# Three plain norms: the first chunk behind each multiplies unnormalised halves, and the roots go on in the banks

## The chip, the cores and the metric

The kernel runs on one core of one Trainium2 chip. The metric is the device time of one execution in microseconds; lower is better.

## The reference

Two blocks of two layers each work on x (512 tokens, width 1024, float32). The first has a latent-attention and RWKV mixer, then a Mamba-2 mixer, each followed by a cross attention to a memory and a gated feed-forward; the second has two layers of a gated attention mixer and a convolved feed-forward. What matters here is the norm ahead of a projection:

```python
def rms_norm(x, g, eps=NORM_EPS):
    xf = x.astype(jnp.float32)
    y = xf * lax.rsqrt(jnp.mean(xf * xf, axis=-1, keepdims=True) + eps)
    return (y * g.astype(jnp.float32)).astype(x.dtype)

def swiglu_ffn(h, norm, w13, w2):
    u = rms_norm(h, norm) @ w13
    return (jax.nn.silu(u[..., :FFN_HIDDEN]) * u[..., FFN_HIDDEN:]) @ w2
```

The root belongs to a token, so it can be multiplied in before or behind the product with W. Three norms are touched: ffn_norm of layer 0 (site 1), od_norm ahead of the Mamba projection (site 2) and ffn_norm of layer 1 (site 3). They have a gain and no shift.

## The kernel before

x is kept transposed: eight tiles of 128 features by 512 tokens. Each projection is a Job, cut into chunks of up to 512 output columns (four tiles, four PSUM banks) and each chunk into slices of 128 input features. For every slice, weights and activations are split into a rounded high half and a low half, and TensorE (L417) runs three terms: high x high, low x high, high x low; with four tiles that is 12 matmuls. ScalarE rounds the weights (L436) four slices ahead of TensorE, once slice s-4 is done, and GpSimd makes their low halves (L440). Chunks take the two groups of four banks in turn; a chunk may start when the one before it in its group has given its banks back (`await_free`). A guest job (od_dt, 32 columns) is run in the middle of od_x, after slice 3 of its second chunk, in the bank group of the first.

What else belongs to a job is its Finish: generators for ScalarE and VectorE. `Stream.walk` writes the order of each queue: at every slice it first rounds weights (ScalarE only), then takes two steps of the pending Finish generators, then one step of a `beside` generator. At the first slice of a job with flush=0 all that is pending is written out first. The queues are in order, so a wait holds up all behind it.

A plain norm (class Rms) follows a job that adds into x (AddToX, chunks of 512, 256 and 256 columns). VectorE adds each tile to x (L987), ScalarE squares it (L703), VectorE folds the squares of tiles 0 to 5 into one (L724). The last chunk is "rushed": tiles 6 and 7 are added and squared by halves (L708). When the job ends, TensorE sums the folded squares (L738) and the halves (L715) with a matrix of ones, runs filler matmuls (`keep_busy`, L239), and transposes the roots so that they stand in a bank as a row for every partition (L746), with more filler behind. Between them VectorE averages (L798), ScalarE takes the root (L753) and VectorE inverts it (L2283 to L2291). VectorE then scales tile after tile by gain and row (L821, L825), ScalarE rounds (L760, L772), VectorE takes the low half (L781); the next job's first chunk follows tile by tile.

The job behind sites 1 and 3 is ffn_up0 (class Gated, eight slices a chunk): ScalarE's sigmoids (L1974), VectorE's products with the banks (L1986, L1991), the rounding (L1979) and the low half (L1995) of the result. After that VectorE has a "rider" with each chunk, a product of mod_w with a vector (L1039 and seven L1044), which TensorE turns by four transposes (L1064) after slice 5 of the next chunk. Behind site 2 come od_x (class Mixed: ScalarE L2104, then twelve taps of a convolution on VectorE, L2123, which read the banks) and its guest od_dt. The xo job ahead of sites 1 and 3 has four slices a chunk, the down job ahead of site 2 has ten.

RowsLater is an older relative: the norm of the cross attention multiplies raw halves, rounded at L848 and with the low half at L852.

## Time and profile before

| | us |
|---|---|
| median of 3 runs | 3366.26 (3365.47 to 3368.86) |
| profiled execution | 3368.29 |
| its span | 3366.4 |
| TensorE busy | 3304.4 (98%) |
| VectorE busy | 1763.8 (52%) |
| ScalarE busy | 1435.9 (43%) |
| GpSimd busy | 1492.0 (44%) |
| mean granted TensorE clock | 0.997 of full speed |

The busy times come from the page of the profile. TensorE's holds its filler and its sums too. The timeline lists the instructions of all engines in order of time, equal neighbours merged, with the idle time ahead of them in brackets.

### The profile page before, as it was taken

How to read it: one execution, taken by the hardware profiler on the slowest of the kernel's cores; microseconds unless marked ns; L12 is line 12 of the kernel's file. 1: busy time of each engine (PE TensorE's matmuls, PEld its weight loads, DVE VectorE, ACT ScalarE, POOL GpSimd, SP SyncE). 2: the span in 40 equal slices, each digit the busy share in tenths (PEclk: the TensorE clock that was granted, in tenths of full speed). 3: DMA queues.
4: the chain of work that ended last, by engine and by line, in shares of the span. 5: the costliest groups of instructions: out<-in, count | busy, mean ns of one | idle time of the engine just before them, and what ended most of it. 6: DMA issues, size and time to landing. Idle time of an engine off the chain costs nothing. (4 is left out here: it accounts for less than half of the span.)

```text
span 3366.4 us, 48377 instructions
## 1 busy us (share of the span) xinstructions
PE 3304.4 (98%) x19096; PEld 2724.3 (81%) x19096; DVE 1763.8 (52%) x3073; ACT 1435.9 (43%) x2918; POOL 1492.0 (44%) x1353
## 2 busy tenths in 40 slices
PE   9999999999998999999999999999999999999999
PEld 7769788888886788888888877888888877888887
DVE  4765675636456664656353376445153186545143
ACT  4662354323355554532333337344343246444343
POOL 3330254454443545354544443445554443444543
PEclk9999999999999999999999999999999999999999
DMA  4210024545221123354533220232323220123331
GB/s 124 75 57 4 27 88 151 194 144 192 85 88 51 42 97 100 101 169 163 170 125 117 82 77 11 75 100 86 102 85 103 92 82 26 51 89 99 100 94 56
DMA packets 233851, 317.79 MB, mean 94 GB/s; under 512 B 8877, under 2 KB 151196, under 8 KB 233628
## 3 DMA queue, kind: packets, MB, share of 16 engines
q1 hardware_dynamic: 204982, 260.50, 24.1%
q10 hardware_dynamic: 28646, 54.22, 4.7%
q8 instruction: 152, 2.49, 0.3%
q14 instruction: 71, 0.58, 0.1%
HBM read 312.59 MB, written 2.10 MB: 93 GB/s over the span
## 5 line engine op out<-in xcount | busy, mean ns | idle before, releaser
L417 PE MATMUL banks<-split,split 128*128 128x512 f32 (+2 forms) x11760 | 2675.2, 388 | 8.1 <-ACT split L436 3.7
L417 PEld LDWEIGHTS banks<-split,split 128*128 128x128 f32 x11760 | 2183.7, 188 | 476.5 <-issue 15.7
L440 POOL TENSOR_TENSOR split<-kept,split 128x512 fp32r<-128x512 f32 (+3 forms) x1174 | 1363.8, 1166 | 1581.1 <-ACT split L436 1578.6
L436 ACT ACTIVATE split<-kept 128x512 fp32r<-128x512 f32 (+3 forms) x1174 | 648.9, 559 | 1436.4 <-PE banks L417 1389.3
L2047 DVE SCALAR_TENSOR_TENSOR work<-banks,kept,work 128x511 f32<-128x511 f32 (+1 forms) x176 | 120.4, 745 | 257.1 <-ACT work L2029 256.3
L1044 DVE SCALAR_TENSOR_TENSOR work<-work,kept 128x512 f32<-128x512 f32 x168 | 195.5, 1164 | 6.0
L989 DVE SCALAR_TENSOR_TENSOR kept<-banks,kept 128x512 f32<-128x512 f32 (+1 forms) x56 | 34.3, 669 | 207.8 <-PE banks L417 207.8
L987 DVE TENSOR_TENSOR kept<-banks,kept 128x512 f32<-128x512 f32 (+1 forms) x72 | 41.1, 625 | 193.2 <-PE banks L417 193.2
L613 DVE COPY work<-banks 128x512 f32<-128x512 f32 (+1 forms) x64 | 37.4, 643 | 187.9 <-PE banks L417 187.9
L1986 DVE TENSOR_TENSOR work<-work,banks 128x512 f32<-128x512 f32 x44 | 28.3, 684 | 165.5 <-ACT work L1974 165.5
L1673 ACT ACTIVATE work<-work 128x128 f32<-128x128 f32 (+3 forms) x160 | 89.5, 560 | 47.0 <-DVE work L1733 46.1
L2123 DVE SCALAR_TENSOR_TENSOR work<-banks,kept,work 128x511 f32<-128x511 f32 (+2 forms) x72 | 49.5, 742 | 58.9 <-ACT work L2104 58.4
L239 PE MATMUL banks<-kept 128*128 128x128 f32 x438 | 60.2, 290 | 12.4 <-PEq L266 10.2
L1600 PE MATMUL banks<-kept,work 128*128 128x128 f32 x400 | 71.0, 275 | 0.6 <-ACT work L1673 0.6
L1733 DVE CUSTOM_DVE_ANT_0 work<-banks,kept 128x128 f32<-128x128 f32 (+3 forms) x96 | 46.8, 487 | 41.6 <-PE banks L1888 21.1
L239 PEld LDWEIGHTS banks<-kept 128*128 128x128 f32 x438 | 55.9, 204 | 15.4 <-issue 13.0
L724 DVE TENSOR_TENSOR work<-work 128x512 f32<-128x512 f32 x66 | 64.0, 969 | 7.5 <-ACT work L703 2.1
L1616 PE MATMUL banks<-work 128*64 128x128 f32 x592 | 61.1, 283 | 0.8 <-DVE work L1744 0.5
L2029 ACT ACTIVATE work<-banks,kept 128x512 f32<-128x512 f32 x88 | 60.9, 771 | 0.0
L1600 PEld LDWEIGHTS banks<-kept,work 128*128 128x128 f32 x400 | 48.7, 140 | 14.9 <-issue 6.2
L3871 PE MATMUL banks<-kept 64*64 64x64 f32 (+1 forms) x1408 | 55.4, 233 | 1.9 <-DVE kept L4106 1.4
L3871 PEld LDWEIGHTS banks<-kept 64*64 64x64 f32 x1408 | 53.0, 134 | 3.5 <-DVE kept L4106 3.5
(460 smaller groups left out, 3106.7 us busy)
## 6 DMA issues: line engine op xcount, KB each, us to landing
work<-in_mod_w ACTq DMA_DIRECT2D x48, 1024.0 KB, 6.5
kept<-in_ffn_w SPq DMA_DIRECT2D x94, 512.0 KB, 4.9
kept<-in_w_up SPq DMA_DIRECT2D x88, 512.0 KB, 4.7
kept<-in_w_in SPq DMA_DIRECT2D x36, 1024.0 KB, 5.0
kept<-in_od_w_in SPq DMA_DIRECT2D x19, 1024.0 KB, 5.2
kept<-in_ffn_w SPq DMA_DIRECT2D x18, 1024.0 KB, 5.4
kept<-in_w_down SPq DMA_DIRECT2D x18, 1024.0 KB, 5.2
kept<-in_ev_w_in SPq DMA_DIRECT2D x8, 1024.0 KB, 5.2
```

The costliest lines, as they stand in the source:

```text
L239: pe.matmul(self.PS[:, bank, 0:P], self.ident, self.ones, start=True, stop=True)
L417: m = pe.matmul(self.bank(q, j), lhs, rhs, start=t == 0 and i == 0, stop=t == job.KT - 1 and i == 2)
L436: act.activation(self.weights(s, 0), self.source(s), ACT.Copy).then_inc(self.rounded, 1)
L440: pool.tensor_tensor(self.weights(s, 1), self.source(s), self.weights(s, 0), ALU.subtract).then_inc(self.k.slices_split, 1)
L724: dve.tensor_tensor(total, total, self.square_at(t), ALU.add).then_inc(self.folded, 1)
L1044: ins = dve.scalar_tensor_tensor(out=self.sum, in0=self.slot[:, t, :], scalar=self.x[:, t:t + 1], in1=self.sum, op0=ALU.mult, op1=ALU.add)
L1600: m = pe.transpose(self.bank(self.TB[u % 2])[:, c * P:(c + 1) * P], self.prob[u % 4][:, c * P:(c + 1) * P], self.k.ident)
L1616: ins = pe.matmul(self.o_bank(h // 2)[i * 64:i * 64 + 64, t * P:(t + 1) * P], self.heads[h + i].v(c), self.probT[(u + i) % 3][:, c * P:(c ...
L1673: act.activation(tile, tile, ACT.Exp, bias=self.top[:, u % 8:u % 8 + 1], scale=-1.0, accum_out=self.total[:, u % 16:u % 16 + 1]).then_inc( ...
L2029: act.activation(self.cv[:, j, :], self.stream.bank(q, j), ACT.Identity, bias=col(self.k, f"conv_b_2{self.l}", at), scale=col(self.k, f"co ...
L2047: return dve.scalar_tensor_tensor(out=v, in0=self.stream.bank(q, j)[:, 0:S - lag], scalar=col(self.k, f"conv_w_2{self.l}{2 - lag}", self.c ...
L3871: m = pe.matmul(PS[half, bank, q * P:q * P + n], lhs(q)[half], rhs(q)[half], start=start, stop=stop)
```

## The change

The three norms become RawFirst. In AddToX each tile of x is now also rounded with its gain and without the root, and VectorE takes its low half; all eight squares are folded, the last chunk is no longer rushed, and nothing of the norm stands between the jobs. The first chunk of the next job multiplies the raw halves. Behind its slice 1 TensorE sums the folded squares, behind slice 3 it transposes the roots, and ScalarE copies the row from its bank to SBUF. From slice 4 on VectorE scales x by gain and that row, ScalarE rounds and VectorE takes the low half, two tiles a slice, for the later chunks; scaling tile t waits until slice t has been multiplied. VectorE multiplies the four finished banks of the first chunk by the row, and the Finish reads them after that. At site 2 the raw halves have places of their own (the low ones where the scaled x goes), and the guest waits for the normed halves. At its core:

```diff
-            terms = (whi, hi(t)), (wlo, hi(t)), (whi, lo(t))
+            high, low = finish.operands(c, hi, lo)
+            terms = (whi, high(t)), (wlo, high(t)), (whi, low(t))
...
+        elif c == 1 and self.raw_first():
+            self.after.await_normed_high(pe, t)
     def ready_low(self, pe, c, t):
         if self.after and c == 0:
             self.after.await_half(pe, t)
+        elif c == 1 and self.raw_first():
+            self.after.await_normed_half(pe, t)
+    def raw_first(self):
+        return isinstance(self.after, RawFirst)
+    def operands(self, c, hi, lo):
+        return self.after.raw if c == 0 and self.raw_first() else (hi, lo)
+    def even_out(self, dve, q, j):
+        bank = self.stream.bank(q, j)
+        self.stream.await_tile(dve, q, j)
+        if j == 0:
+            dve.wait_ge(self.after.kept, 1)
+        dve.tensor_tensor(bank, bank, self.after.row, ALU.mult).then_inc(self.after.evened, 1)
+    def await_even(self, eng, q, c, j):
+        if c == 0 and self.raw_first():
+            eng.wait_ge(self.after.evened, j + 1)
+        else:
+            self.stream.await_tile(eng, q, j)
...
+class RawFirst(Rms):
+    SUM, ROOT, SPREAD, SCALE = 1, 1, 3, 4
+    def __init__(self, k, T, src, gain, halves, squares_at, n_squares, rows_at, tmp, n_tmp, dim, raw=None):
+        super().__init__(k, T, src, gain, halves, squares_at, n_squares, rows_at, tmp, n_tmp, dim)
+        self.raw = raw or halves
+        self.row = self.sq[:, n_squares - 1, :]
+    def signals(self, st):
+        super().signals(st)
+        self.kept, self.evened = st.signals(2)
+    def round(self, act, t):
+        act.activation(self.raw[0](t), self.src(t), ACT.Identity, scale=self.gain(t)).then_inc(self.rounded, 1)
+    def rest(self, dve, t):
+        dve.wait_ge(self.rounded, t + 1)
+        dve.scalar_tensor_tensor(out=self.raw[1](t), in0=self.src(t), scalar=self.gain(t), in1=self.raw[0](t), op0=ALU.mult,
+                                 op1=ALU.subtract).then_inc(self.halved, 1)
+    def used_by(self, stream, job, bank):
+        self.stream, self.bank_at = stream, bank
+        self.slice0 = next(s for s, one in enumerate(stream.slices) if one[1] is job)
+    def beside(self, pe, t):
+        if t == self.SUM:
+            self.sum_folded(pe, self.k.PS[:, self.bank_at, :])
+        if t == self.SPREAD:
+            self.spread_roots(pe, self.k.PS[:, self.bank_at + 1, :])
+    def normed_round(self, act, t):
+        act.wait_ge(self.scaled, t + 1)
+        act.activation(self.hi(t), self.tmp(t % self.n_tmp), ACT.Copy).then_inc(self.rounded, 1)
+    def normed_rest(self, dve, t):
+        dve.wait_ge(self.rounded, self.T + t + 1)
+        dve.tensor_tensor(self.lo(t), self.tmp(t % self.n_tmp), self.hi(t), ALU.subtract).then_inc(self.halved, 1)
+    def normed_scale(self, dve, t):
+        self.stream.await_slice(dve, self.slice0 + t)
+        if t >= self.n_tmp:
+            dve.wait_ge(self.halved, self.T + t - self.n_tmp + 1)
+        dve.scalar_tensor_tensor(out=self.tmp(t % self.n_tmp), in0=self.src(t), scalar=self.gain(t), in1=self.row,
+                                 op0=ALU.mult, op1=ALU.mult).then_inc(self.scaled, 1)
+    def scalar_beside(self, act):
+        for _ in range(self.slice0):
+            yield
+        for i in range(self.SCALE + self.T // 2 + 1):
+            if i == self.ROOT:
+                self.root_of(act)
+            if i == self.SPREAD:
+                act.wait_ge(self.spread, 1)
+                act.activation(self.row, self.rows, ACT.Copy).then_inc(self.kept, 1)
+            for t in range(2 * (i - self.SCALE), min(2 * (i - self.SCALE + 1), self.T)):
+                if t >= 0:
+                    self.normed_round(act, t)
+            yield
+    def vector_beside(self, dve, link):
+        for _ in range(self.slice0):
+            yield
+        for i in range(self.SCALE + self.T // 2 + 1):
+            if i == self.ROOT:
+                self.roots(dve, link)
+            if i == self.SCALE:
+                dve.wait_ge(self.kept, 1)
+            for t in range(2 * (i - self.SCALE), 2 * (i - self.SCALE + 1)):
+                if 0 <= t < self.T:
+                    self.normed_scale(dve, t)
+                if 1 <= t <= self.T:
+                    self.normed_rest(dve, t - 1)
+            yield
+    def await_normed_high(self, eng, t):
+        eng.wait_ge(self.rounded, self.T + t + 1)
+    def await_normed_half(self, eng, t):
+        eng.wait_ge(self.halved, self.T + t + 1)
...
+        self.raw = isinstance(rms, RawFirst)
+        self.folded = rms.T if rms_later or self.raw else self.FOLDED
         if rms:
             rms.fold_first(self.folded)
-            rms.by_halves = not rms_later
+            rms.by_halves = not rms_later and not self.raw
...
-        if self.rms and not self.rms_later and c == len(self.job.widths) - 1:
-            eng.wait_ge(self.rms.scaled, self.rms.T)
+        if self.rms and c == len(self.job.widths) - 1:
+            if self.raw:
+                eng.wait_ge(self.rms.kept, 1)
+            elif not self.rms_later:
+                eng.wait_ge(self.rms.scaled, self.rms.T)
...
+                self.rms.round(act, self.first(c) + j)
+                yield
...
+                self.rms.rest(dve, self.first(c) + j)
+                yield
...
+            self.after.beside(pe, t)
...
+                self.even_out(dve, q, j)
+            yield
...
+    stream = Stream(k, [(xo, AddToX(k, rms=rms), *o_halves), *ffn_jobs(k, plan, l, rms, rms_next), *tail],
+                    HALVES_AT, opened=Opened.N, beside=Besides([rms, *([rms_next] if l == 0 else [])]))
+    rms.used_by(stream, up, stream.free_banks(xo))
+    if l == 0:
+        rms_next.used_by(stream, plan["od_x"], stream.free_banks(down))
+    stream.run()
```

A new `Besides` steps the RawFirst generators (two in layer 0, one in layer 1) once a slice. In AddToX the new steps (round, rest) come behind the adds, squares and folds of each chunk.

## Rows read from the trace of the kernel before

**Rows 1.** The page: busy time (x instructions), and the costliest line with its idle.

```profile
PE 3304.4 (98%) x19096; PEld 2724.3 (81%) x19096; DVE 1763.8 (52%) x3073; ACT 1435.9 (43%) x2918; POOL 1492.0 (44%) x1353
...
L417 PE MATMUL banks<-split,split 128*128 128x512 f32 (+2 forms) x11760 | 2675.2, 388 | 8.1 <-ACT split L436 3.7
```

**Rows 2.** Timeline, site 1: start, us, engine line op out<-in xcount [idle <-releaser].

```profile
526.67 1.05 PE L738 MATMUL banks<-kept,work 128*128 128x128 f32 x8
...
527.56 1.95 PE L715 MATMUL banks<-kept,work 128*128 128x128 f32 x16
...
530.80 0.65 PE L746 MATMUL banks<-kept,work 128*128 128x128 f32 x4
...
531.29 1.28 PE L239 MATMUL banks<-kept 128*128 128x128 f32 x10
...
532.69 27.48 PE L417 MATMUL banks<-split,split 128*128 128x512 f32 x120
```

**Rows 3.** Timeline around site 2.

```profile
897.93 1.05 PE L738 MATMUL banks<-kept,work 128*128 128x128 f32 x8
...
903.95 46.42 PE L417 MATMUL banks<-split,split 128*128 128x512 f32 x203
```

**Rows 4.** Timeline: VectorE at an earlier raw norm (437), then ahead of site 1.

```profile
437.18 12.74 DVE L852 SCALAR_TENSOR_TENSOR split<-kept,split 128x512 fp32r<-128x512 f32 x8
...
515.31 2.48 DVE L987 TENSOR_TENSOR kept<-banks,kept 128x512 f32<-128x512 f32 x4 [11.48 <-PE banks L417]
...
518.84 1.84 DVE L724 TENSOR_TENSOR work<-work 128x512 f32<-128x512 f32 x2 [0.46 <-DVE work L724]
...
521.20 1.29 DVE L987 TENSOR_TENSOR kept<-banks,kept 128x512 f32<-128x512 f32 x2 [0.52 <-PE banks L417]
...
523.06 0.62 ACT L436 ACTIVATE split<-kept 128x512 fp32r<-128x512 f32 x1
...
528.67 1.27 POOL L440 TENSOR_TENSOR split<-kept,split 128x512 fp32r<-128x512 f32 x1 [0.35 <-ACT split L436]
```

**Rows 5.** Timeline: scalings of the first chunk at site 1.

```profile
533.32 0.74 DVE L825 SCALAR_TENSOR_TENSOR work<-kept,banks 128x512 f32<-128x512 f32 x1
...
534.58 0.74 DVE L825 SCALAR_TENSOR_TENSOR work<-kept,banks 128x512 f32<-128x512 f32 x1
```

**Rows 6.** Timeline behind the first chunk of site 1.

```profile
554.77 0.63 ACT L436 ACTIVATE split<-kept 128x512 fp32r<-128x512 f32 x1 [2.09 <-PE banks L417]
...
557.35 1.28 DVE L1986 TENSOR_TENSOR work<-work,banks 128x512 f32<-128x512 f32 x2 [15.59 <-ACT work L1974]
...
558.55 1.27 DVE L1991 TENSOR_TENSOR work<-work,banks 128x512 f32<-128x512 f32 x2
...
561.14 1.53 DVE L1039 TENSOR_SCALAR work<-work,kept 128x512 f32<-128x512 f32 x1
562.70 8.28 DVE L1044 SCALAR_TENSOR_TENSOR work<-work,kept 128x512 f32<-128x512 f32 x7
...
571.13 0.63 PE L1064 MATMUL banks<-kept,work 128*128 128x128 f32 x4
```

**Rows 7.** Timeline behind the first chunk of site 2.

```profile
926.54 2.77 ACT L2104 ACTIVATE work<-banks,kept 128x512 f32<-128x512 f32 x4
...
927.33 8.26 DVE L2123 SCALAR_TENSOR_TENSOR work<-banks,kept,work 128x511 f32<-128x511 f32 x12 [14.32 <-ACT work L2104]
```

**Rows 8.** PE's timeline; a stretch: us, busy by engine, PEclk, DMA share, GB/s.

```profile
40.41 5.47 PE L417 MATMUL banks<-split,split 128*128 128x512 f32 x12
...
1064.65 0.41 PE L4385 MATMUL banks<-split,split 128*128 128x384 f32 x1 [2.62 <-issue]
...
1067.00:1068.00 1.00, 1.00 (x12) 1.00 (x12) 1.00 (x3) 0.00 (x0) 0.00 (x0) 0.51 0.07 16
...
1139.32 1.58 PE L239 MATMUL banks<-kept 128*128 128x128 f32 x12 [2.45 <-PEq L266]
1140.65 5.71 PE L417 MATMUL banks<-split,split 128*128 128x512 f32 x24
```

More of the change, by code:

```diff
@@ L358, in __init__, with free_banks @@
             self.done_by.append(whole)
+    def free_banks(self, job):
+        last = self.first_chunk(job) + len(job.widths) - 1
+        assert job.tiles(len(job.widths) - 1) <= 2
+        return self.groups[last] * 4 + 2
     def first_chunk(self, job):
@@ new lines, with __init__, signals, scalar @@
+class Besides(Part):
+    def __init__(self, norms):
+        self.norms = norms
+    def signals(self, st):
+        pass
+    def scalar(self, act, q, c):
+        works = [norm.scalar_beside(act) for norm in self.norms]
+        while any([next(work, 0) is None for work in works]):
+            yield
+    def vector(self, dve, link, q, c):
+        works = [norm.vector_beside(dve, link) for norm in self.norms]
+        while any([next(work, 0) is None for work in works]):
+            yield
+    def more(self, block):
+        pass
@@ L923, in rushes @@
     def rushes(self, c):
-        return self.rms is not None and not self.rms_later and c == len(self.job.widths) - 1
+        return self.rms is not None and self.rms.by_halves and c == len(self.job.widths) - 1
     def await_free(self, eng, c):
         eng.wait_ge(self.added, self.first(c + 1) + (self.job.tiles(c) if self.rushes(c) else 0))
-        if self.rms and not self.rms_later and c == len(self.job.widths) - 1:
-            eng.wait_ge(self.rms.scaled, self.rms.T)
+        if self.rms and c == len(self.job.widths) - 1:
[3 more added lines that the diff above has]
+                eng.wait_ge(self.rms.scaled, self.rms.T)
         if self.rider and c == 0:
@@ L946, in tensor_end @@
             self.rms.sums_bank = self.sums_bank()
-        elif self.rms:
+        elif self.rms and not self.raw:
             q2 = self.stream.first_chunk(self.job) + 2
@@ L972, in scalar @@
             yield
+        if self.raw:
+            for j in range(self.job.tiles(c)):
+                self.rms.round(act, self.first(c) + j)
+                yield
         if self.rider and c == 0:
@@ L976, in scalar @@
             yield from self.rms.finish_scalar(act)
-        if self.rms and not self.rms_later and c == len(self.job.widths) - 2:
+        if self.rms and self.rms.by_halves and c == len(self.job.widths) - 2:
             act.activation(self.k.idle, self.k.ones[:, 0:1], ACT.Sqrt)
@@ L996, in vector @@
                 yield
+        if self.raw:
+            for j in range(self.job.tiles(c)):
+                self.rms.rest(dve, self.first(c) + j)
+                yield
         if self.rider and c == 0:
             yield from self.rider.vector(dve, link, self.RIDES, self.k.PS[:, q % 2 * 4, :])
-        if self.rms and c == len(self.job.widths) - 1:
+        if self.rms and not self.raw and c == len(self.job.widths) - 1:
             yield from self.rms.finish_vector(dve, link)
@@ L1960, in tensor @@
     def tensor(self, pe, c, t):
+        if c == 0 and self.raw_first():
+            self.after.beside(pe, t)
         if c >= 1 and t == self.job.KT - 3:
@@ L1983, in vector @@
     def vector(self, dve, link, q, c):
+        if c == 0 and self.raw_first():
+            for j in range(4):
+                self.even_out(dve, q, j)
+            yield
         for p in range(2):
@@ L2113, in scalar, with tensor @@
                 yield
+    def tensor(self, pe, c, t):
+        if c == 0 and self.raw_first():
+            self.after.beside(pe, t)
     def vector(self, dve, link, q, c):
+        if c == 0 and self.raw_first():
+            for j in range(4):
+                self.even_out(dve, q, j)
+            yield
         for lag in range(1, 4):
@@ L2940, in cross_attention @@
            opening=[opening], beside=mem, closing=[attend], idle_first=0 if l == 0 else 6, early=SLOTS if l == 0 else 1).run()
-    rms = x_norm(k, lambda t: col(k, f"ffn_norm{l}", t), split_tiles(k, A_WORK, A_H), at=HID_AT + 8 * S)
+    rms = x_norm(k, lambda t: col(k, f"ffn_norm{l}", t), split_tiles(k, A_WORK, A_H), at=HID_AT + 8 * S,
+                 raw=True)
     if l == 0:
-        rms_next = x_norm(k, lambda t: col(k, "od_norm", t), odd_halves(k), dst=k.H)
+        rms_next = x_norm(k, lambda t: col(k, "od_norm", t), odd_halves(k), dst=k.H, raw=split_tiles(k, A_WORK, A_H))
         xbc = k.view(A_WORK, XBC // P, S)
@@ L2948, in cross_attention @@
         mixed = Mixed(k, xbc, SCRATCH_AT + 7 * S, after=rms_next, flush=0)
-        tail = [(plan["od_x"], mixed, *h), (plan["od_dt"], Steps(k, dt, tmp, cum, odd_spread(k), at_tile(43), at_tile(59)), *h),
+        tail = [(plan["od_x"], mixed, *h), (plan["od_dt"], Steps(k, dt, tmp, cum, odd_spread(k), at_tile(43), at_tile(59), rms_next), *h),
                 (plan["od_xbc"], Mixed(k, xbc, SCRATCH_AT + 7 * S, tile0=8, before=mixed), *h)]
@@ L2974, in split_tiles, with x_norm @@
     return lambda t: hi[:, t, :], lambda t: lo[:, t, :]
-def x_norm(k, gain, halves, shift=None, at=SCRATCH_AT, dst=None, n_squares=4):
+def x_norm(k, gain, halves, shift=None, at=SCRATCH_AT, dst=None, n_squares=4, raw=None):
     if dst is None:
@@ L2983, in x_norm @@
         tmp, n_tmp = (lambda i: dst[:, i, :]), DT
+    if raw:
+        return RawFirst(k, DT, lambda t: k.X[:, t, :], gain, halves, at, n_squares, at + n_squares * S, tmp, n_tmp, D,
+                        raw=None if raw is True else raw)
     return Rms(k, DT, lambda t: k.X[:, t, :], gain, halves, at, n_squares, at + n_squares * S, tmp, n_tmp, D, shift=shift)
@@ L4189, with __init__ @@
 class Steps(Finish):
-    def __init__(self, k, dt, tmp, cum, spread, rest_at, rounded_at, after=None, flush=None):
-        self.k, self.after, self.flush, self.spread_with = k, after, flush, spread
+    def __init__(self, k, dt, tmp, cum, spread, rest_at, rounded_at, normed):
+        self.k, self.normed, self.spread_with = k, normed, spread
         self.dt, self.tmp, self.cum = (v[0:SSM_H, :] for v in (dt, tmp, cum))
@@ L4199, in signals, with ready, ready_low @@
         self.freed, self.begun, self.bent = st.signals(3)
+    def ready(self, pe, c, t):
+        self.normed.await_normed_high(pe, t)
+    def ready_low(self, pe, c, t):
+        self.normed.await_normed_half(pe, t)
     def scalar(self, act, q, c):
```

10 lines of the change are left out of this document (4 added, 6 removed).

## The prediction

> **What bounds the kernel now.** The page first: TensorE is busy 98% of the span, and its main line, L417, waits 8.1 us in 11760 matmuls [rows 1]. So time can only be won where TensorE does something that the reference doesn't need, and lost where it is made to wait. Then the timeline around the first norm that the change touches (site 1, ffn_norm0). The last matmul of the output projection gives way to the sum of the folded squares at 526.67, the half sums start at 527.56, the spreading transposes at 530.80, filler at 531.29, and the next chunk's first matmul comes at 532.69 [rows 2]. That is 6.02 us in which TensorE sums, spreads and runs filler. Site 2 (od_norm) has the same gap, 897.93 to 903.95 [rows 3], and site 3 (ffn_norm1) repeats it at 1414.64 to 1420.67. A slice of 12 matmuls costs 2.72 us (120 in 27.48, less the drain of the last [rows 2]). Last, the timeline of the first chunk behind each site, for what VectorE owes when that chunk ends; here lies the answer.
>
> **What goes.** At each site TensorE no longer stands between two jobs: 3 x 6.02 = 18.1 us. It keeps the folded sum, 527.56 - 526.67 = 0.89, now behind slice 1 of the chunk, and the four transposes, 531.29 - 530.80 = 0.49 [rows 2], now behind slice 3: 1.38 a site. **Gross gain 3 x 4.64 = 13.9 us.** The Sqrt behind the averages loses the early load of its table, but from the end of the sums to the transposes the whole root takes about 1.3 us now [rows 2], and two slices, 5.4 us, lie between them after the change: free, and it would cost something only if it grew fourfold. The raw halves of tiles 0 to 5 are made while the projection still runs, so slice 0 can start at once.
>
> **What comes in, before the boundary (sites 1 and 3).** VectorE gets a second subtraction per x tile (8 of the form of L852) and two more folds. The xo job has only four slices a chunk, so its last two chunks last 10.9 us. I lay VectorE's queue out for site 1: the four adds start at 515.31 and take 0.62 each, the folds 0.92 each beside GpSimd [rows 4], which ends them at 520.7 (as now). New: four raw rests. Alone such an operation takes 0.74 (L825's form [rows 5]); beside a GpSimd that never pauses L852 takes 12.74 / 8 = 1.59 [rows 4]. GpSimd works here on 256-wide slices with pauses, so I take 1.0, nearest to the folds of this place: 524.7. Only then the adds of tiles 4 and 5, to 526.0 (now they are done by 522.5). ScalarE squares tile 5 by 526.6, and only then rounds the chunk's first weights, which now happens at 523.06 [rows 4]. TensorE wants them at 526.67: about 1.0 us late, part of it for the low half, which GpSimd makes in 1.27 more [rows 4]. Behind that, two folds, two rests, two adds and the last two folds end near 533.2, against TensorE's arrival at the sum at 533.1. So 1.0 us a site. Bounds: 0.2 with every rest at 0.74; 4.9 with every rest and fold at 1.6. Site 2 has ten slices a chunk: the same work ends 7 us before the boundary, and tiles 6 and 7 are folded by +4 us (even at the 1.6 us price) against an arrival at +5.4: nothing.
>
> Operations of VectorE that read two tensors of SBUF stretch beside GpSimd (1.59 against 0.74 [rows 4, 5]), while those with a bank as source stay at 0.69 to 0.74 (L825 [rows 5], L2123 [rows 7]). The new scaling reads its row from SBUF, the old one read it from a bank. The Trainium skill's SBUF — State Buffer, "Who interferes with whom", speaks here against the change: a VectorE instruction with two SBUF inputs and a GpSimd one that reads SBUF exclude each other for a whole instruction. By that rule the scalings join the exposed kind; on the path are scale 6 and 7, 2 x 0.85 = 1.7 a site if GpSimd runs beside both, and nothing by the rows of the bank.
>
> **What comes in, behind the boundary (sites 1 and 3).** Eight scalings and eight low halves, now done while TensorE runs the chunk itself, move to slices 4 to 8. Two scalings and two roundings go with a slice, and ScalarE rounds only after it has seen slice t end, so tiles 0 to 5 are ready by the chunk's end, about 0.6 us ahead of it: free. Call that end E; at site 1 now E = 532.69 + 8 x 2.72 = 554.45. VectorE is idle from there to its first gating product at 557.35, E+2.9 [rows 6]; the four new products of a bank with the row of roots, 0.62 to 0.65 each by the adds' rows [rows 4], fit: free. They sit ahead of the sigmoids only by one tile each, and ScalarE's table load covers that.
> Not free is what the order puts next: scale 6, rest 5, scale 7, rest 6 between the gating products and the second products at 558.55, and rest 7 ahead of the mod_w work of the rider (L1039 at 561.14, L1044). A scaling with its rest takes 1.26 now (533.32 to 534.58 [rows 5]); GpSimd is mostly idle in that moment, since ScalarE, waiting for VectorE, hands it nothing. Two pairs are 2.5, with 0.3 for the exchange with ScalarE, rest 7 0.7 to 0.8: **3.6 us later**. The rider's eight products now run from 561.14 to 570.98, and TensorE's L1064, which needs their sum, starts at 571.13, when the chunk's sixth slice has ended at 554.45 + 6 x 2.72 = 570.77, plus a little: the two arrive within 0.3 us of each other [rows 6]. There is no slack. 3.6 us of VectorE turn into 3.6 us of TensorE at site 1 and again at site 3 (the same rows recur at 1459.09). Bounds: 0 if the rider should wait for something that is not late; 7.5 if all five, at 1.6 (+3.9), collide. The delay ends there: the rider would be through by about 575, and the next chunk, whose work VectorE waits for then, ends some 5 us later.
>
> **Site 2.** No rider, but the od_dt guest wants chunk 0's banks after three slices plus one of chunk 1, at E + 4 x 2.72 = E+10.9, and takes them when VectorE's twelve taps are through. E = 903.95 + 21.76 = 925.71. Now the taps start at E+1.6 and end at 935.59, E+9.9 [rows 7]: slack 1.0. After: the four bank products end at E+2.2, so the taps start 0.6 later, two pairs come in after the first two taps (2.9 with the exchange), rest 7 after six (0.7): +4.2, **3.2 us of waiting**. Bounds: 2.5 (pairs at 1.26 and no exchange) and 5.5 (four of five at 1.3 to 1.6).
>
> **The sum.** 13.9 - 2 x 1.0 - 2 x 3.6 - 3.2 = **1.5 us faster**; against the profiled execution, 3368.29 (span 3366.4 and 1.9 around it), that is 3366.8. The profiled execution lies 2.0 above the median of 3366.26, which becomes **3364.8**. A measurement of this kernel tells some 0.2%, 6.7 us, from no change.
>
> **Rivals.**
> A. The rider isn't late: the pairs hide in VectorE's waits for ScalarE, or TensorE's own 1 us of lateness covers them. For it: VectorE idles 2.9 us behind E. Against it: that idle time is spent before the pairs are reached, by the order of the queue. Gain 13.9 - 2.0 - 3.2 = 8.7, or 3357.6. If nothing is late anywhere, 13.9: 3352.4.
> B. The pre-boundary queue at GpSimd's full price: 4.9 in place of 1.0, twice: 1.5 - 7.8 = -6.3, or 3372.6. For it: L852's eight rows. Against it: GpSimd's pauses, and the folds' 0.92 in this very stretch.
> C. The clock falls in the new waits; this ends on the slower side. Now the boundary is filled with matmuls; the new waits of 3.2 to 3.6 us are bare. The bare wait of 2.45 is followed by full rate (24 matmuls in 5.71 [rows 8]); the one of 2.62, in sparse work, is followed by a granted clock of 0.51, that is 1.2 GHz in place of 2.4 [rows 8]. At that level 12 matmuls took 5.47 in place of 2.72: 2.75 lost [rows 8]. My waits lie just above the longest that is known to be harmless. Three falls cost 8.3: 1.5 - 8.3 = -6.8, or 3373.1. It turns the sign from one such fall on, and it passes 0.2% when three come or when two come with B. The page TensorE: Matmul & The Clock Gate of the Trainium skill ("What's actually happening") describes two levels granted by recent activity; rows 8 agree, and my price is theirs.
>
> **How the numbers follow.** Forecast 0.50 (own range 3361 to 3369: the two unknown rates of VectorE), A 0.15 and nothing late 0.05, B 0.12, C 0.18, of which two thirds pass 0.2%. Faster by over 0.2%: A, nothing late, and a little of the forecast's edge, 0.22. Slower: 0.12 of C and a little of B, 0.13. The same: 0.65. The range leaves out nothing late, half of C's far side and what lies past B: 3357 to 3373.5.
>
> **What would show it.** At each site L417 follows L417 without L715 or L239 between, and L738 comes after 24 more matmuls. Right: waits of L417 for L436 or L440 near 1 us at the first slice of the up0 job; the L1064 of the first rider 3 to 4 us late, released by L1044; the first guest matmul 3 us late, released by L2123. Wrong: L1064 on time (A), granted clock under 1.0 in the slices after a wait (C), the scalings at 0.74 beside GpSimd (the port does not matter), or a wait at the transposes (the root chain is not free).

## The result, and the profile after

| | before | after |
|---|---|---|
| median, same chip | 3366.65 us (5 runs) | 3380.93 us (5 runs, 3379.22 to 3384.7) |
| profiled execution | 3368.29 | 3379.22 |
| its span | 3366.4 | 3377.4 |
| mean granted TensorE clock | 0.997 | 0.995 |

The ratio is 1.0041 [1.0029, 1.0052]: 14.3 us slower, where 1.5 us faster was forecast, and outside the range. The direction was wrong too. The profiled executions differ by 11.0 us of span.

The page after, lines that answer to [rows 1]:

```profile
PE 3298.0 (98%) x18982; PEld 2712.5 (80%) x18982; DVE 1815.7 (54%) x3106; ACT 1448.7 (43%) x2933; POOL 1499.9 (44%) x1353
...
L424 PE MATMUL banks<-split,split 128*128 128x512 f32 (+2 forms) x11760 | 2683.5, 389 | 13.0 <-DVE work L2292 4.5
```

L424 is the old L417. The same 11760 matmuls are busy 8.3 us longer (2683.5 against 2675.2) and wait 4.9 us longer. The mean clock, 0.995 against 0.997, hardly moves, but the busy time of unchanged work hints at a lower clock, and the stretches below show it. The waits of TensorE, by line and releaser (sum, times, longest), hold three large entries that belong to the change:

```profile
PE banks L1219 <- DVE work L1199: 10.6, 2, 5.3
...
PE banks L424 <- DVE work L2292: 4.5, 1, 4.5
...
PE banks L771 <- DVE work L757: 2.3, 2, 1.2
```

L1219 is the rider (old L1064) at sites 1 and 3, L424 behind L2292 the guest at site 2, L771 (old L738) the sum of the folded squares. TensorE's timeline at site 1, to be held against [rows 2, 6]:

```profile
501.46 23.12 PE L424 MATMUL banks<-split,split 128*128 128x512 f32 x100
524.94 4.84 PE L424 MATMUL banks<-split,split 128*128 128x512 f32 x20 [0.36 <-POOL split L447]
530.95 1.16 PE L771 MATMUL banks<-kept,work 128*128 128x128 f32 x8 [1.17 <-DVE work L757]
531.86 5.72 PE L424 MATMUL banks<-split,split 128*128 128x512 f32 x24
537.42 0.60 PE L779 MATMUL banks<-kept,work 128*128 128x128 f32 x4
537.77 27.48 PE L424 MATMUL banks<-split,split 128*128 128x512 f32 x120
570.54 1.09 PE L1219 MATMUL banks<-kept,work 128*128 128x128 f32 x4 [5.29 <-DVE work L1199]
571.28 19.05 PE L424 MATMUL banks<-split,split 128*128 128x512 f32 x72
```

The gap of 6 us is gone: L424 follows L424 over the boundary (it lies in the row of 501.46), with the sum and the transposes between its slices. What came in stands in the brackets (0.36, 1.17, 5.29), and in the last row: 72 matmuls in 19.05, where six slices should take about 16.3. The stretches of one microsecond around the end of the rider's wait say why (busy share and count for PE, PEld, DVE, ACT and POOL, then PEclk, the granted clock; the last two numbers are the DMA's):

```profile
569.00:570.00 1.00, 0.00 (x0) 0.00 (x0) 1.00 (x1) 0.00 (x0) 0.85 (x1) 0.83 1.03 393
570.00:571.00 1.00, 0.46 (x3) 0.49 (x4) 0.40 (x1) 0.15 (x1) 0.00 (x0) 0.50 1.08 356
...
573.00:574.00 1.00, 1.00 (x4) 0.71 (x4) 0.00 (x0) 0.00 (x0) 0.00 (x0) 0.50 1.08 373
...
577.00:578.00 1.00, 1.00 (x6) 0.83 (x5) 0.00 (x0) 0.36 (x1) 0.57 (x1) 1.00 0.00 0
```

The clock falls in the last microsecond of the wait (0.83 is the mean of a stretch in which it fell), stays at 0.50 (1.2 GHz), with four matmuls a microsecond, and is back at 1.00. It is rival C: the wait, and then the clock. The Trainium skill's page TensorE: Matmul & The Clock Gate ("What's actually happening") describes just these two levels, with the lower one granted after TensorE was idle; the trace agrees, 0.50 behind the wait of 5.29 and 1.00 before and after.

VectorE at site 1, around the end of the first chunk, shows why the rider waits. E, counted as in the prediction, is 537.77 + 4 x 2.72 = 548.65. L956 is the scaling (here of tiles 3, 4 and 5), L594 the product of a finished bank with the row, L2147 the first gating product, L2156 the low half of that job's result, L950 the last low half of the normed tiles (rest 7), L1194 and L1199 the rider's eight products; POOL L447 makes the low halves of the weights:

```profile
544.24 1.59 POOL L447 TENSOR_TENSOR split<-kept,split 128x512 fp32r<-128x512 f32 x1 [1.37 <-ACT split L443]
544.61 1.77 DVE L956 SCALAR_TENSOR_TENSOR work<-kept,work 128x512 f32<-128x512 f32 x1
...
546.90 0.74 DVE L956 SCALAR_TENSOR_TENSOR work<-kept,work 128x512 f32<-128x512 f32 x1
...
547.64 1.75 POOL L447 TENSOR_TENSOR split<-kept,split 128x512 fp32r<-128x512 f32 x1 [1.81 <-ACT split L443]
...
548.17 1.78 DVE L956 SCALAR_TENSOR_TENSOR work<-kept,work 128x512 f32<-128x512 f32 x1
...
550.47 2.48 DVE L594 TENSOR_TENSOR banks<-banks,work 128x512 f32<-128x512 f32 x4
...
553.07 1.28 DVE L2147 TENSOR_TENSOR work<-work,banks 128x512 f32<-128x512 f32 x2
...
558.18 1.81 DVE L2156 TENSOR_TENSOR split<-work,split 128x512 fp32r<-128x512 f32 x2
559.92 1.77 DVE L950 TENSOR_TENSOR split<-work,split 128x512 fp32r<-128x512 f32 x1
561.61 1.51 DVE L1194 TENSOR_SCALAR work<-work,kept 128x512 f32<-128x512 f32 x1
563.16 7.24 DVE L1199 SCALAR_TENSOR_TENSOR work<-work,kept 128x512 f32<-128x512 f32 x7
```

**The ledger.** Take the time between two points of TensorE that lie outside all that the change moves: from the last filler ahead of the stage to the third rider at sites 1 and 3, from the twelfth rider to the filler at the stage's end at site 2. In the profiled executions that is 111.51, 184.77 and 111.50 us before, and 117.07, 186.04 and 116.55 after: +5.56, +1.27, +5.05, in all +11.9. The parts: -4.64 x 3; waits of 2 x (0.36 + 1.17 + 5.29) + 4.53 = 18.2; and the low clock at the three large waits, 3.41, 1.70, 3.42 (one minus PEclk, summed over stretches of 1 us), 8.5. Sum 12.8. That counts 1.7 twice: at each site the clock fell before the wait was over, and the low stretch inside the waits makes 0.4, 0.3 and 1.0 of the 8.5. Without it the clock is 6.9 and the sum 11.1, 0.8 short of what was measured.

### The profile page after: what moved, and what is told of

It reads as the page before. It is cut to its first block and busy times, and to the rows that moved or that the text cites. A ratio compares the mean times of both kernels' runs of the same rounds, so it can differ in the third digit from the quotient of the medians.

```text
span 3377.4 us, 48250 instructions
## 1 busy us (share of the span) xinstructions
PE 3298.0 (98%) x18982; PEld 2712.5 (80%) x18982; DVE 1815.7 (54%) x3106; ACT 1448.7 (43%) x2933; POOL 1499.9 (44%) x1353
## 5 line engine op out<-in xcount | busy, mean ns | idle before, releaser
L424 PE MATMUL banks<-split,split 128*128 128x512 f32 (+2 forms) x11760 | 2683.5, 389 | 13.0 <-DVE work L2292 4.5
L424 PEld LDWEIGHTS banks<-split,split 128*128 128x128 f32 x11760 | 2187.0, 188 | 485.2 <-issue 21.0
L447 POOL TENSOR_TENSOR split<-kept,split 128x512 fp32r<-128x512 f32 (+3 forms) x1174 | 1371.7, 1173 | 1583.5 <-ACT split L443 1580.9
L1199 DVE SCALAR_TENSOR_TENSOR work<-work,kept 128x512 f32<-128x512 f32 x168 | 193.4, 1151 | 6.0
L2147 DVE TENSOR_TENSOR work<-work,banks 128x512 f32<-128x512 f32 x44 | 28.3, 684 | 139.7 <-ACT work L2131 139.5
L757 DVE TENSOR_TENSOR work<-work 128x512 f32<-128x512 f32 x72 | 71.8, 997 | 8.5 <-ACT work L736 2.1
L2292 DVE SCALAR_TENSOR_TENSOR work<-banks,kept,work 128x511 f32<-128x511 f32 (+2 forms) x72 | 49.6, 742 | 44.6 <-ACT work L2265 44.1
L239 PE MATMUL banks<-kept 128*128 128x128 f32 x372 | 51.2, 290 | 12.4 <-PEq L266 10.2
L239 PEld LDWEIGHTS banks<-kept 128*128 128x128 f32 x372 | 47.3, 203 | 15.4 <-issue 13.0
```

Source lines behind the costliest of these rows:

```text
L239: pe.matmul(self.PS[:, bank, 0:P], self.ident, self.ones, start=True, stop=True)
L424: m = pe.matmul(self.bank(q, j), lhs, rhs, start=t == 0 and i == 0, stop=t == job.KT - 1 and i == 2)
L447: pool.tensor_tensor(self.weights(s, 1), self.source(s), self.weights(s, 0), ALU.subtract).then_inc(self.k.slices_split, 1)
L757: dve.tensor_tensor(total, total, self.square_at(t), ALU.add).then_inc(self.folded, 1)
L1199: ins = dve.scalar_tensor_tensor(out=self.sum, in0=self.slot[:, t, :], scalar=self.x[:, t:t + 1], in1=self.sum, op0=ALU.mult, op1=ALU.add)
```

## The experiments

Times by site are from each profiled execution, between the same points. "Clock" is one minus PEclk, summed over the low stretches that begin in or just behind the large waits of sites 1, 2 and 3; as in the ledger, the part that passes while TensorE still waits is in it.

| kernel | site 1 | site 2 | site 3 | clock | median | ratio to before |
|---|---|---|---|---|---|---|
| before | 111.51 | 184.77 | 111.50 | 0 | 3366.65 (5 runs) | |
| before again | 111.53 | 184.81 | 111.51 | 0 | 3364.71 (1 run) | |
| after | 117.07 | 186.04 | 116.55 | 3.41, 1.70, 3.42 | 3380.93 | 1.0041 [1.0029, 1.0052] |
| after again | 115.63 | 188.26 | 115.85 | 1.71, 3.42, 1.71 | 3382.72 (1 run) | |
| site 2 only | 111.50 | 188.40 | 111.50 | 0, 3.42, 0 | 3372.42 | 1.0013 [1.0003, 1.0023] |
| filler | 114.26 | 185.91 | 114.24 | 0, 1.71, 0 | 3375.42 | 1.0023 [1.0013, 1.0033] |
| slack | 110.96 | 184.27 | 112.60 | 0, 1.71, 1.71 | 3367.08 | 1.0002 [0.9992, 1.0011] |
| late rests | 116.28 | 188.44 | 116.64 | 3.41, 3.41, 3.42 | 3381.91 | 1.0045 [1.003, 1.006] |
| bank row | 114.44 | 184.79 | 114.24 | 1.7 each | 3374.63 | 1.0021 [1.0012, 1.003] |
| behind the rider | 114.30 | 188.62 | 114.24 | 1.7, 3.41, 1.71 | 3378.84 | 1.0026 [1.0015, 1.0036] |
| slack and bank | 110.76 | 182.23 | 110.78 | none | 3366.19 | 0.9993 [0.9984, 1.0001] |
| all three | 108.47 | 182.23 | 108.43 | none | 3360.37 | 0.9977 [0.9968, 0.9985] |
| rider at slice 6 | 107.85 | 182.20 | 107.86 | none | 3359.80 | 0.9976 [0.9967, 0.9986] |

The medians of before on the three chips of the experiments were 3366.91 (first four kernels from "site 2 only"), 3368.22 (next four) and 3367.0 (the last and the two repeats). In the four profiles with 3.4 at site 2 (after again, site 2 only, late rests, behind the rider) a further fall of 1.7 lies at 1038 to 1044, near the end of that stage and behind none of the waits named here; it is in their time for site 2 and not in the clock column.

**Site 2 only.** The feed-forward norms are plain again.

```diff
-    rms = x_norm(k, ..., at=HID_AT + 8 * S, raw=True)
+    rms = x_norm(k, ..., at=HID_AT + 8 * S)
-                    ..., beside=Besides([rms, *([rms_next] if l == 0 else [])]))
+                    ..., beside=Besides([rms_next] if l == 0 else []))
```

> Sites 1 and 3 keep the old norm, only od_norm takes the raw first chunk. Theory T (each site costs its own waits and the clock that falls behind them, and the sites add up): site 2 gives 4.6 us back, waits 4.5 for the taps and loses 1.7 at the low clock, so 1 to 2 us slower than before, about 3368; at sites 1 and 3 the trace shows the old gap of 6.0. Rival D (the loss is spread over the whole kernel, its second block too, by whatever changed in the program): a good part of the 14 us stays, 3372 or more.

Sites 1 and 3 return to 111.50. Site 2 costs 3.63: -4.64, the guest's wait of 4.53, 2.5 of clock behind it (3.42 less what passed in the wait) and the fall at 1038, up to 1.7, sum 2.4 to 4.1. At that wait the clock falls with nothing changed at the other sites:

```profile
929.00:930.00 1.00, 0.30 (x2) 0.00 (x0) 1.00 (x3) 0.00 (x0) 0.00 (x0) 1.00 0.00 0
...
936.00:937.00 1.00, 1.00 (x4) 0.45 (x3) 0.00 (x0) 0.23 (x1) 0.09 (x1) 0.50 0.00 0
```

By its number this run fell to rival D: 3372.42 is 5.5 above its before, where 1 to 2 were expected. The sites hold 3.6 of it. The profile shows most of the rest behind site 3, where the kernel is the same and two falls of 1.7, at 2004 and 2028, stand where before has none. So the sites account for most of the loss, and not for all of it.

**Filler in the rider's wait** at sites 1 and 3. It takes no wait away; it keeps TensorE occupied in it.

```diff
         pe.wait_ge(self.made, 2 * c + 2)
+        if c == 0 and self.raw_first():
+            self.k.keep_busy(pe, q % 2 * 4 + 1, 20)
```

> The changed kernel with 20 filler matmuls (about 5 us) ahead of TensorE's wait for the first rider at sites 1 and 3; it would wait there anyway. Theory T: the granted clock stays at 1.00 behind both waits and 2 x 3.4 us come back: about 3374. Rival Q (only the waits cost, the slices behind them are late because ScalarE and GpSimd fed no weights meanwhile): no gain, 3381, and the slices behind the wait last as long as in the changed kernel.

TensorE's timeline: the wait of 5.29 has become 4.62 of filler and 0.76 of wait.

```profile
566.34 4.62 PE L239 MATMUL banks<-kept 128*128 128x128 f32 x40
571.72 0.66 PE L1219 MATMUL banks<-kept,work 128*128 128x128 f32 x4 [0.76 <-DVE work L1199]
572.14 18.19 PE L424 MATMUL banks<-split,split 128*128 128x512 f32 x79
```

The stretch behind it runs at full clock (0.50 at the same place after):

```profile
572.00:573.00 1.00, 1.00 (x8) 0.87 (x7) 0.58 (x1) 0.63 (x1) 0.17 (x1) 1.00 1.03 328
```

The sites take 2.8 and 2.3 us less than after, where 3.4 each was expected; 0.4 and 1.0 of after's 3.4 had passed in the wait. The dependence is as late as before, and no low stretch is left at sites 1 and 3, while site 2, which got no filler, has its wait of 4.53 and a fall as in after. So this part of the loss is the clock's alone: C is shown. What is left at these sites, +2.75 each, is in the main waits: 0.36 + 1.17 + 5.38 - 4.64 = 2.3.

**Slack.** The first rider is turned behind the last slice of the next chunk in place of the sixth; the guest waits for the taps of the first bank instead of all twelve.

```diff
-                freeing.await_free(pe, freed)
+                if job.hosted and isinstance(freeing, Mixed):
+                    pe.wait_ge(freeing.tapped, freeing.first(freed) + 1)
+                else:
+                    freeing.await_free(pe, freed)
...
-        if c >= 1 and t == self.job.KT - 3:
+        if c >= 1 and t == self.job.KT - 1 - (0 if c == 1 and self.raw_first() else 2):
```

> The changed kernel, but TensorE turns the first rider after slice 7 of the second chunk in place of slice 5, and the guest waits for the taps of tile 0 alone, the only bank it writes. VectorE's queue is as in the changed kernel. Theory T: the wait of 5.3 becomes 1.4 (now for the rider's sum at the next chunk's start), the guest's 4.5 becomes 2.4, and no clock falls: 2 x 7.3 + 3.8 = 18.4 us less, about 3362.5, faster than before. Rival Q: only the waits shrink, 2 x 3.9 + 2.1 = 9.9, about 3371. Rival S (VectorE's late queue pushes on whatever comes next): the wait moves to the next chunk's banks at full length, 3377 or more.

```profile
571.28 0.63 PE L1222 MATMUL banks<-kept,work 128*128 128x128 f32 x4
573.72 16.57 PE L427 MATMUL banks<-split,split 128*128 128x512 f32 x72 [1.82 <-DVE kept L1216]
```

The rider itself no longer waits, but there is a new wait of 1.82 right behind it: VectorE adds up the turned rider (L1216) before it gives the next chunk its banks. It was expected at 1.4, with no fall of the clock and 3362.5 in all. The guest waits 2.57. With all other work left as in after, two deadlines moved bring back nearly all of the 14 us (3367.08 beside 3366.91). The clock fell behind the 2.57, and 1.5 us behind one of the two waits of 1.82.

**Late rests.** The raw low halves of a chunk are made behind the folds of the next.

```diff
-        if self.raw:
-            for j in range(self.job.tiles(c)):
-                self.rms.rest(dve, self.first(c) + j)
+        if self.raw and c >= 1:
+            last = c == len(self.job.widths) - 1
+            for t in range(self.first(c - 1), self.first(c + 1) if last else self.first(c)):
+                self.rms.rest(dve, t)
```

> The changed kernel, but VectorE takes the raw low halves of a chunk's tiles one chunk later, behind the adds and folds of the next chunk. Theory T: the waits of 0.35 and 1.2 us at the first slice and at the sum of sites 1 and 3 vanish, the wait for the rider stays 5.3: 3.0 us less, about 3378. Rival: the rests that now come after the boundary push VectorE's later queue, and the rider's wait grows by what is won, 3381.

A miss: 3378 was expected. The wait of 0.36 is gone, but the one at the sum grew from 1.17 to 1.77, and the rider's stayed at 5.30, so the rival's account does not hold either. Out of the way of the adds, the four rests fall beside GpSimd's 512-wide halves, and all four take 1.72 each where they took 0.92:

```profile
522.71 6.88 DVE L930 SCALAR_TENSOR_TENSOR split<-kept,split 128x512 fp32r<-128x512 f32 x4
...
532.42 1.16 PE L771 MATMUL banks<-kept,work 128*128 128x128 f32 x8 [1.77 <-DVE work L757]
```

**Bank row.** Scalings 0 to 5 read the row of roots from its bank, where it stands anyway; the bank is given on only when these six are done.

```diff
-        dve.scalar_tensor_tensor(..., in1=self.row,
+        dve.scalar_tensor_tensor(..., in1=self.rows if t < 6 else self.row,
...
                 eng.wait_ge(self.rms.kept, 1)
+                eng.wait_ge(self.rms.scaled, 6)
```

> The changed kernel, but the scalings of tiles 0 to 5 read the row of roots from its bank, not from the copy in SBUF (tiles 6, 7 and the bank products still read the copy). Contention (a scaling with two SBUF inputs waits for GpSimd's instruction): the 1.77 us scalings become 0.74, the first bank product starts about 1.2 us earlier against the chunk's end, and each of the waits for rider and guest is 1.2 us shorter (4.1, 3.3, 4.1); 3 to 5 us less than the changed kernel, 3376 to 3378. Rival (VectorE is paced by ScalarE's roundings there, not by GpSimd): the scalings are shorter but the first bank product starts where it did, and the waits stay 5.3 and 4.5.

The line of the scaling at sites 1 and 3, minimum, median and maximum in ns; first this kernel's form with the bank, then after's form with both inputs in SBUF:

```profile
L956 DVE SCALAR_TENSOR_TENSOR work<-kept,banks x12: 732/734/748, 539.4 to 1439.6; 128x512 f32<-128x512 f32 x12
```

```profile
L956 DVE SCALAR_TENSOR_TENSOR work<-kept,work x16: 739/743/1778, 538.8 to 1450.8; 128x512 f32<-128x512 f32 x16
```

The same operation on the same data never exceeds 748 with one input in a bank, and reaches 1778 without. GpSimd works beside it here too. The timeline:

```profile
544.85 1.60 POOL L447 TENSOR_TENSOR split<-kept,split 128x512 fp32r<-128x512 f32 x1 [1.37 <-ACT split L443]
...
545.21 0.73 DVE L956 SCALAR_TENSOR_TENSOR work<-kept,banks 128x512 f32<-128x512 f32 x1
...
549.88 2.48 DVE L594 TENSOR_TENSOR banks<-banks,work 128x512 f32<-128x512 f32 x4
...
569.73 1.03 PE L1220 MATMUL banks<-kept,work 128*128 128x128 f32 x4 [3.87 <-DVE work L1200]
```

Here E is 538.38 + 10.88 = 549.26: the bank products start at E+0.6, not E+1.8, and the rider's wait is 3.87 in place of 5.29. The rival, that ScalarE paces VectorE there, is out: the products did start earlier. Two low halves behind the scalings (L950) went from 0.68 to 1.12, so 1.2 of the 2.1 us is won, not all. At site 2 the guest's wait is 3.33, and at site 3 the rider's 3.86.

These waits are those of the prediction within 0.3 (3.6, 3.2, 3.6), in part by luck: from the first gating product to the rider's start is 560.80 - 552.27 = 8.53, 4.7 more than before and not 3.6, and the rider's own products are 1.05 shorter than before. And the kernel, though below the 3376 to 3378 expected, is still 6.4 us slower than its before, because the clock fell at all three waits, 1.7 each. The two falls of 3.4 in after are of 1.7 here, which after again shows without any edit: that part of the gain on after need not be an effect of the bank.

**Behind the rider.** The last two steps of the generator come five slices later, behind the rider's products.

```diff
+    def steps(self):
+        n = self.SCALE + self.T // 2 + 1
+        ...
+        return [*range(n - 2), *[None] * 5, n - 2, n - 1]
```

> The changed kernel, but at sites 1 and 3 scale 6, rest 5, scale 7, rest 6 and rest 7 (with ScalarE's two roundings) stand behind the rider's eight products in the queues. Theory T (those five operations, some 4.3 us with the stretch of rest 7, and the late start of 1.2 us make the wait of 5.3): the rider's wait falls to about 1 us, a new wait of 1 to 2 us for the high half of tile 6 comes behind it, and no clock falls there: 2 x (3 + 3.4), about 3368 to 3370. Rival (the late start and the rider's own contention make it): the wait stays over 3 us.

```profile
569.10 1.22 PE L424 MATMUL banks<-split,split 128*128 128x512 f32 x4 [3.59 <-DVE split L952]
```

A miss: 3368 to 3370 was expected. The edit took more along than meant: the low half of tile 5 belongs to these steps, and TensorE wants it at slice 5, so one wait replaced another and the total says little. The timeline still prices the five operations. The rider's products end at 567.78 here, with E = 538.94 + 10.88 = 549.82: E+18.0. In after they end at 563.16 + 7.24 = 570.40, E+21.75. The five are 3.8 us at the rider's end (its start moves by 4.7, from E+13.0 to E+8.2, but its own products take 1.0 longer), and even without them the rider is 1.4 later than before (E+16.5).

**Slack and bank** is both of those edits together.

> The rider turned after slice 7 and the guest on tile 0 alone, as before, together with the scalings that read the bank. Theory T: the waits of 1.8 at sites 1 and 3 fall to 0.6, the guest's 2.6 to 1.4, no clock falls behind them: sites 1 and 3 each 2.5 us and site 2 3.2 us shorter than in the kernel before, about 3359 to 3361. Rival: falls of the clock behind the remaining waits of 1 to 2 us take part of it, 3363 to 3366.

It is 2.0 us less than before by its median, and the interval reaches 1; the sites, in one profile, are -0.75, -2.5 and -0.7. No clock fell behind their waits, of which the longest is now 1.73. Expected were 0.6 for that wait and 3359 to 3361; the number is that of the rival's range (3363 to 3366), its reason, falls behind the waits left, is not. The 1.73 hardly changed from 1.82, though VectorE was 1.2 earlier: turned so late, the rider's sum follows TensorE's own transposes. Outside the sites this profile, the slowest of the eleven runs, lost 13.7 us in falls, the first of before 8.5.

**All three** adds a split of the raw rests: 0 and 1 behind the second chunk's folds, 2 and 3 behind the third's, 4 to 7 behind the roots, where VectorE is idle.

```diff
             if i == self.ROOT:
                 self.roots(dve, link)
+                for t in range(4, self.T):
+                    self.rest(dve, t)
...
-        if self.raw:
-            for j in range(self.job.tiles(c)):
-                self.rms.rest(dve, self.first(c) + j)
+        if self.raw and c >= 1:
+            for t in range(2 * (c - 1), 2 * c):
+                self.rms.rest(dve, t)
```

> As the one above, and the raw low halves are spread: tiles 0, 1 behind the second xo chunk's folds, 2, 3 behind the last chunk's, 4 to 7 behind the roots. Theory T: the waits of 0.35 and 1.2 us ahead of the sum vanish at sites 1 and 3 too, 3 us less: 3356 to 3358. Rival: VectorE's queue is only pushed on, and the rider's wait takes it back, 3359 to 3361.

```profile
529.49 1.05 PE L774 MATMUL banks<-kept,work 128*128 128x128 f32 x8
530.29 5.70 PE L427 MATMUL banks<-split,split 128*128 128x512 f32 x24
535.83 0.60 PE L782 MATMUL banks<-kept,work 128*128 128x128 f32 x4
536.19 32.92 PE L427 MATMUL banks<-split,split 128*128 128x512 f32 x144
568.95 0.60 PE L1225 MATMUL banks<-kept,work 128*128 128x128 f32 x4
571.30 3.91 PE L427 MATMUL banks<-split,split 128*128 128x512 f32 x16 [1.75 <-DVE kept L1219]
```

No wait is left ahead of the sum or at the boundary. Site 1: 111.51 - 4.64 + 1.75 = 108.62; measured 108.47. The sum takes 530.29 - 529.49 = 0.80 and the transposes 536.19 - 535.83 = 0.36, so the gross gain of 4.64 was right to 0.2. This version beats both kernels: 3360.37, 7.9 below before, with no fall at the sites. Expected were 3356 to 3358; 3360.37 lies in the rival's 3359 to 3361, but the trace speaks against its reason: the wait at the rider is not longer than in "slack and bank", 1.75 against 1.73.

**Before and after again** are second profiles of the two kernels, to see what moves from one execution to the next.

> The kernel before, profiled once more. If the falls of the clock outside the three sites move from execution to execution, its list of low stretches (3.4 us at 39 to 46, 1.7 at 1049 and at 1067 in the first profile) changes, while sites 1, 2, 3 last 111.5, 184.8, 111.5 us again. If the falls belong to the kernel, the list is the same and the changed kernels' falls at 201, 1143 and 2003 to 2034 come from the change.

> The changed kernel once more. Theory T: the falls behind the waits of 5.3 are there again with 3.4 us at low clock each, since so long a wait leaves no choice; behind the guest's wait of 4.5 one fall or two (1.7 or 3.4, as in the runs so far). Rival: falls behind the waits are chance, and at least one of sites 1 and 3 has none.

The waits repeat (2 of 5.3, one of 4.5). Falls came at all three both times, against the rival, but their size changes, against the 3.4 expected at each wait of 5.3: 3.41, 1.70, 3.42 the first time, 1.71, 3.42, 1.71 the second. Undisturbed, the sites of before repeat within 0.04. The falls of before lie at 19, 40, 1050 and 1067 in its first profile and at 19, 1046 and 1060 in its second (3.4 at 40 and at 1060, 1.7 at the others), so those outside the sites move from execution to execution too.

**Rider at slice 6** is all three, with the first rider one slice earlier, so that its sum is ready when the next chunk wants its banks.

```diff
-        if c >= 1 and t == self.job.KT - 1 - (0 if c == 1 and self.raw_first() else 2):
+        if c >= 1 and t == self.job.KT - 2 - (0 if c == 1 and self.raw_first() else 1):
```

> As the last of the kernels with all mends, but the first rider is turned after slice 6. By the traces the rider's sum ends at E+20.1 and TensorE is there at E+19.1: a wait of 1.0 in place of 1.75 and none at the next chunk. Sites 1 and 3 0.7 us shorter each, 3359. Rival: the waits add up, one of 1.0 and one of 1.0 at the next chunk's banks, 3361.

```profile
PE banks L1225 <- DVE work L1205: 2.4, 2, 1.2
```

The wait of 1.75 became one of 1.20 at the rider (1.0 was expected), and the sites are 0.6 shorter each; the median, 3359.80, can't be told from 3360.37.

## Why the prediction was wrong, step by step

- **What goes** held. The gap vanished, the root chain cost nothing, the order of the pieces was as told.
- **Before the boundary**: right mechanism, 1.0 predicted, 0.36 + 1.17 = 1.53 measured. The place was another: 1.0 had been put at the first slice, where 0.36 came, and 0.1 at the sum, where 1.17 came. Rests 0 to 3 took 3.69 / 4 = 0.92 as assumed, but 4 and 5 took 3.16 / 2 = 1.58, beside the 512-wide halves of the next job's weights; the estimate used GpSimd's pace of the job that was ending. "All three" took these waits away. Rival B's 4.9 did not come.
- **"Tiles 0 to 5 are ready by the chunk's end, about 0.6 us ahead of it: free"**: this step failed. It priced the scalings at their bank form's 0.74. Tiles 3 and 5 took 1.77 and 1.78, the bank products started at E+1.8 and the first gating product came at E+4.4 instead of E+2.9: 1.5 us late, on the path. The prediction had named the exposure of the scalings and looked for it only at scale 6 and 7, which ran at 0.74. The tiles that suffered were those called hidden. "Bank row" shows it: products at E+0.6, gating at 552.27, E+3.0. The Trainium skill's SBUF — State Buffer, "Who interferes with whom", which the prediction had named, says that a VectorE instruction with two SBUF inputs and a GpSimd one that reads SBUF get in each other's way; the trace agrees: 1.77 against 0.74 with both inputs in SBUF beside GpSimd, never over 0.75 with one in a bank.
- **The five operations**, 3.6, were mis-sized: from the first gating product to the start of the rider's work is 561.61 - 553.07 = 8.54 now against 561.14 - 557.35 = 3.79 before [rows 6], 4.75 in all. The pairs took the 2.5 that was said; rest 7 took 1.77 for 0.75, and the low halves ahead of it 1.81 for 1.29 (L1995 before). The rider's own products were 1.05 shorter than before, so 3.7 of the 4.75 reach its end; "behind the rider" has 3.8. Together: 1.5 + 4.75 - 1.05 = 5.2, the wait of 5.29. The upper bound of 7.5 was worked out too low as well: five operations at 1.6 are 4.7 more than two pairs of 1.26 and a rest of 0.75, not 3.9. That there was no slack was right, and "slack" shows that this, not the amount of work, decided.
- **Site 2**, 3.2: 4.53, of which "bank row" gives back 1.2; the same failed step.
- **The clock (rival C)**: this step failed too, and by itself. The sum put the clock at nothing, and C had 0.18, because waits of 3.2 to 3.6 lay just above a harmless 2.45. The waits became 4.5 and 5.3, and at every one of them the clock fell. But longer waits were not needed for it: in "bank row", with 3.87, 3.33 and 3.86, close to the waits predicted, it fell at all three, and the kernel was 6.4 slower than before and not 1.5 faster. "Filler" shows the clock's part alone, 2.8 and 2.3 at sites 1 and 3.
- **The sum** in the prediction's terms, at the sites: 13.9 - 3.1 - 10.6 - 4.5 = 4.3 slower from waits, and 6.9 more from the clock behind them. Against 1.5 faster, 5.8 came through durations and 6.9 through the clock. C's price of 2.75 a fall was near: at 1.7 or 3.4, it lies between the two sizes.

What stays open: the median moved by 14.3, the sites by 11.9 and 12.0 in the two profiles of after. Behind site 3, where the change touches nothing, the rest of the span takes 1862.8 and 1862.7 in the profiles of before, and 1864.8, 1866.0, 1864.4 and 1867.5 in those of after, after again, all three and the rider at slice 6. Single falls of 1.7 at 201 to 204, 1131 to 1146, 1992 to 2037 and 2797 to 2820 are in most changed kernels and in neither profile of before; behind site 3 all changed kernels take 1.6 to 4.7 us more than before, and the one or two falls there are a good part of it. Ahead of site 1, the first profile of before lost 5.1 to the clock and that of after 1.7, which is why the spans differ by 11.0 only. Why the falls outside the sites come where they do, and whether the change brings them, was not found. Nor was it shown how long a bare wait may be: 2.45 was harmless and 1.75 too, yet one of 2.57 and one of two of 1.82 were followed by a fall.

## What to carry to other kernels

A dependence that arrives with 0.3 us to spare is the first thing to move when work is put on its engine: here shifting two such deadlines was worth nearly the whole loss, before any of the work was made faster. Price work that is "hidden" at its worst measured form, not at its best; an underestimate there lands on the path, and the lower clock behind a bare wait of several microseconds can cost 1.7 to 3.4 us more: here all bare waits of 3.3 to 5.3 at the sites had it. So a forecast that ends in bare waits on TensorE needs the clock in its sum. A VectorE operand that stands in a bank is better read from there than from a copy in SBUF where GpSimd works beside.

## What the runs showed of the hardware

- A VectorE operation of 128x512 with two inputs in SBUF takes 0.74 alone and 1.77 when GpSimd's 128x512 subtraction overlaps it, whose own time goes from 1.29 to 1.59 or 1.75. So a single overlap cost VectorE more than the 1.59 of the back-to-back row at 437.18 [rows 4].
- A fall at a wait came to either 1.7 or 3.4 us, the size changing between two executions of the same kernel with the same waits; a part of it passes in the wait itself. Small filler matmuls in the wait (40 in 4.62 us) were enough to keep 1.00.
- Products in place in PSUM with one input in SBUF took 2.48 / 4 = 0.62 per bank, beside TensorE at work and GpSimd at work alike.
